# Reading the bias table back ahead of two weight preparations, and one weight remainder ahead of a residual update

## The reference

```python
h = h + 0.5 * swiglu(rms_norm(h, norm_ffn1), w_ffn1_in, w_ffn1_out)
u = rms_norm(h, norm_mix)
proj = u @ w_in
aq, ak, av, rq, rf, ri, rg, ga, gb = jnp.split(proj, splits, axis=-1)

# attention: 8 heads over a window of 128, with a bias by distance
bias = rel_table[bucket]                    # [128, 256, 8] from a [32, 8] table
s = jnp.where(valid, einsum(q, k) * 64 ** -0.5 + bias, -inf)
probs = exp(s - m) / (sum(exp(s - m)) + exp(sink - m));  att = probs @ v

# recurrence: f = lb + (1 - lb) * sigmoid(rf); S_t = diag(f_t) S_{t-1} + (1 - f_t) ri_t^T
rec = rms_norm(hgrn2(rq, rf, ri, lb), rec_norm) * sigmoid(rg)
merged = sigmoid(ga) * (att @ w_att_proj) + sigmoid(gb) * (rec @ w_rec_proj)
h = h + merged @ w_out
```

## Time and profile before

| | |
|---|---|
| median of three runs (lowest, highest) | 1578.72 us (1577.44, 1582.83) |
| the profiled execution's own time | 1577.44 us |
| its span in the trace | 1575.6 us |
| mean granted clock of TensorE | 0.962 of full speed |
| busy: TensorE, VectorE, ScalarE, GpSimd | 93%, 56%, 38%, 10% |

### The profile page before, as it was taken

How to read it: one execution, slowest core, us unless ns; L and a number is a source line. 1 busy time by engine, 2 the same in 40 slices (tenths; PEclk the granted TensorE clock), 3 DMA queues, 4 the chain that set the end, 5 groups by cost and what they waited for, 6 DMA issues and landing times.

```text
span 1575.6 us, 25429 instructions
## 1 busy us (share of the span) xinstructions
PE 1472.2 (93%) x10722; PEld 1385.5 (88%) x10722; DVE 879.6 (56%) x1154; ACT 595.4 (38%) x712; POOL 160.3 (10%) x149
## 2 busy tenths in 40 slices
PE   5999997899999999999989998999989889999997
PEld 5999997898899999988878878999988468999997
DVE  4656564674256565731564215866764263776765
ACT  3434343354034544421234112444442154444443
POOL 0000000132000000511011000000050042000014
PEclk9999998999999999999989769999999899999998
DMA  8555547632345555534300023555543412455540
GB/s 267 198 186 186 187 146 167 199 121 94 121 166 169 186 186 186 162 111 136 121 1 1 1 72 128 175 187 186 186 138 115 137 35 81 161 187 186 186 135 27
DMA packets 167216, 221.34 MB, mean 140 GB/s; under 512 B 5452, under 2 KB 148037, under 8 KB 167013
## 3 DMA queue, kind: packets, MB, share of 16 engines
q1 hardware_dynamic: 163564, 216.46, 41.8%
q10 hardware_dynamic: 3576, 3.81, 1.4%
HBM read 217.49 MB, written 2.62 MB: 140 GB/s over the span
## 4 chain that ended last, share of the span: by engine, by line
PE 80%; DVE 9%; ACT 4%; DMA 2%; issue 2%; POOL 1%; ACTq 0%; POOLq 0%; SPq 0%; DVEq 0%
PE ps L846 34%; PE ps L882 14%; PE ps L977 6%; PE ps L822 5%; DMA weight_bays<-in_w_in 2%; PE ps L959 2%; PE ps L1268 1%; PE ps L832 1%; DVE x_second_part L2038 1%; PE ps L1389 1%; PE ps L1405 1%; PE ps L806 1%; PE ps L1263 1%; PE ps L948 1%; PE ps L1417 1%
## 5 line engine op out<-in xcount | busy, mean ns | idle before, releaser
L2134 DVE TENSOR_TENSOR weights_second_parts<-weight_bays,weights_first_parts 128x2048 fp32r<-128x2048 f32 x132 | 301.0, 2289 | 172.4 <-ACT weights_first_parts L1526 172.0
L1526 ACT ACTIVATE weights_first_parts<-weight_bays 128x2048 fp32r<-128x2048 f32 x132 | 252.0, 1917 | 300.7 <-PE ps L846 190.1
L846 PE MATMUL ps<-x_first_part,weights_first_parts 128*128 128x256 f32 x1488 | 209.8, 284 | 1.7 <-DVE weights_second_parts L2134 1.7
L846 PE MATMUL ps<-x_second_part,weights_first_parts 128*128 128x256 f32 x1488 | 209.2, 284 | 0.0
L846 PE MATMUL ps<-x_first_part,weights_second_parts 128*128 128x256 f32 x1488 | 206.5, 282 | 0.0
L846 PEld LDWEIGHTS ps<-x_first_part,weights_first_parts 128*128 128x128 f32 x1488 | 191.3, 191 | 2.3 <-ACT weights_first_parts L1526 1.9
L846 PEld LDWEIGHTS ps<-x_second_part,weights_first_parts 128*128 128x128 f32 x1488 | 192.3, 191 | 0.0
L846 PEld LDWEIGHTS ps<-x_first_part,weights_second_parts 128*128 128x128 f32 x1488 | 189.6, 190 | 0.0
L882 PE MATMUL ps<-hidden_first_part,weights_first_parts 128*128 128x256 f32 x704 | 141.2, 282 | 5.4 <-ACT weights_first_parts L1526 3.7
L882 PE MATMUL ps<-hidden_second_part,weights_first_parts 128*128 128x256 f32 x704 | 141.2, 282 | 0.0
L882 PE MATMUL ps<-hidden_first_part,weights_second_parts 128*128 128x256 f32 x704 | 139.2, 278 | 0.0
(11 more groups left out here) (400 smaller groups left out, 2170.2 us busy)
## 6 DMA issues: line engine op xcount, KB each, us to landing
weight_bays<-in_w_ffn_in SPq DMA_DIRECT2D x44, 1024.0 KB, 5.1
weight_bays<-in_ffn_w_in SPq DMA_DIRECT2D x44, 1024.0 KB, 5.0
weight_bays<-in_w_ffn_out SPq DMA_DIRECT2D x22, 1024.0 KB, 5.0
weight_bays<-in_ffn_w_out SPq DMA_DIRECT2D x22, 1024.0 KB, 5.0
weight_bays<-in_w_in SPq DMA_DIRECT2D x19, 1024.0 KB, 5.7
weight_bays<-in_hyb_w_in SPq DMA_DIRECT2D x13, 1024.0 KB, 5.2
weight_bays<-in_ple_w_gate SPq DMA_DIRECT2D x8, 1024.0 KB, 5.2
weight_bays<-in_w_out SPq DMA_DIRECT2D x4, 1024.0 KB, 5.0
```

The costliest lines, as they stand in the source:

```text
L846: mm = nc.tensor.matmul(dst, w[:, k, j * P:(j + 1) * P], x[:, k], start=(n + k == 0), stop=(n == 2 and k == KD - 1))
L1526: nc.scalar.activation(hi, raw, ACT.Copy).then_inc(*w_hi_ready.inc(f, g, kind, of - g))
L2134: v.tensor_tensor(lo, raw, hi, ALU.subtract).then_inc(*w_lo_d.inc(f, g, kind, of - g))
```

## The change

Two sequences are written in another order; no instruction is added, removed or altered.

On ScalarE, in the body of `mix1`, the wait on `tab_out` and the two DMAs that read the bias back move from behind `prep(6)` and the keeping of ri's first half to ahead of `prep(4)`. On VectorE the remainder of chunk 1 moves from behind the mixer's factors to ahead of the update of h.

```diff
                     keep(fT[:, 2 * n:2 * n + 2], n, ("rf", n), "rf", n, func=ACT.Sigmoid)
-                prep(4)
-                prep(5)
-                prep(6)
-                keep(vR[:, :, 0:256], 0, ("ri", 0), "ri", 0)
                 act.wait_ge(tab_out.sem, 16)
                 shifted = [bass.AP(...) for o, n in ((0, 256), (P, P))]
                 act.dma_start(bias[:, :, 0:256], shifted[0]).then_inc(bias_in.sem, 16)
                 act.dma_start(bias[:, :, 256:384], shifted[1]).then_inc(bias_in.sem, 16)
-                prep(7)
-                keep(vR[:, :, 256:512], 1, ("ri", 1), "ri", 1)
+                prep(4)
+                prep(5)
+                for n in range(2):
+                    prep(6 + n)
+                    keep(vR[:, :, n * 256:(n + 1) * 256], n, ("ri", n), "ri", n)
                 act.wait_ge(*rec_d.at("f"))
...
             ffn("ffn1", False)
             rest_of_mix(0)
+            rest_of_mix(1)
             arrive("mix1", added("ffn1", 0.5, ("ffn1", 3 * GROUPS - 1)))
             factors("mix1", b=0)
-            rest_of_mix(1)
             split_x("mix1", lambda k: col("norm_mix", k), 1)
```

## The result

The changed kernel takes 1599.76 us, the median of four runs (1598.96 to 1600.10), against 1580.78 for the kernel before in the same comparison (1577.44 to 1585.67). The ratio is 1.0117, with a 95% interval of 1.0087 to 1.0147: slower by 19 us where 14.4 were forecast, and outside the range of 1587 to 1598. The profiled execution has 1596.38 us and a span of 1594.4, 18.8 more than the span of before, at a mean granted clock of 0.952 instead of 0.962.

The account below looks back on a forecast made before the run. TensorE's matmuls were taken to hold most of the chain, a weight chunk's landing 2%. ScalarE's 12.5 and VectorE's 1.9 us summed to +14.4, giving 1592.5 us from bases of 1577.44 and 1578.72; range 1587 to 1598.

Parts of the forecast that it names:

- The stop on ScalarE's wait: Ahead of `prep(4)`, ScalarE waits for the table's write until about 265.9 us; chunk 4 starts at 271.4; +12.5 us.
- The restart after a longer stop: Chunk 4, first after the stop, pays the low clock once as chunk 6 did: 7.67 us instead of 5.66.
- the third rival: At the restart in the mixer, the clock stays at 1.2 GHz for both ri chunks: 9.3 us more, 1601; 6%.
- Of this edit 1.85 us arrive at the end: VectorE's remainder of chunk 1 ahead of the update of h delays the table's write by 1.85 us.
- The base and the range: The +14.4 us was put on 1577.44 (profiled execution) and 1578.72 (median), giving 1592.5; range 1587 to 1598 us.
- +18: Upper end of the forecast's step once release, hand-overs, VectorE's term and restart vary; the lower end is +10.5.
- The first rival: The table's write ends sooner: break-even at 20 us; under about 10 us chunk 6's 8.7 us stop goes, 1571; 4%.
- No gain from reading early: Scores using the bias come after chunk 10 in both orders, so reading it back earlier serves nobody.
- +16.4: The sum if ScalarE's release came up to 2 us behind the write's last packet, by the skill's page; not adopted.

Follow-up runs that it names:

- e8_wait_only: The changed kernel with the two reads of the bias moved back behind ri's second half, the wait left ahead of `prep(4)`: 1597.79 us, ratio 1.0084.
- e7_wide_after: The changed kernel with the table's write made from 16 partitions in place of 8, the same bytes: 1579.87 us, ratio 0.9983 against the kernel before.
- e6_filled_less: The changed kernel with the embedding's second pair computed twice, filling TensorE's wait ahead of the sums: 1592.70 us, ratio 1.0065 against the kernel before.
- e4_wide_write: The kernel before with the table's write made from 16 partitions in place of 8, the same bytes: 1570.62 us, ratio 0.9923.

## Why the prediction was wrong in size and right in kind

- **The stop on ScalarE's wait: right.** Release, issues, preparation and restart came as written: 35.08 us from the write's issue to the read (34.99 in the row of before, and 34.87 to the release assumed), 1.15 for the issues and the hand-over (1.1), 4.38 to the first matmul (4.38), 7.52 for the first chunk (7.67). +12.54 for +12.5. `e8_wait_only` has the wait itself as the releaser, and in `e7_wide_after` the stop shrank by as much as the write.
- **The restart after a longer stop: right.** After 21 us of standing still the first chunk took 7.52 us, after 8.7 us 7.67, after 4.37 us (`e7_wide_after`) 7.26, where 5.66 is a chunk at full clock; the third rival falls. Its figure of 1601 is near the measured time by chance.
- **"Of this edit 1.85 us arrive at the end": the step that failed.** The term was mis-sized. The shift of the sums was there (TensorE waits 1.73 us for them), but the sum took the stretch behind it, of sums, bias product, embedding and spread, at the durations of one execution of before, in which the granted clock was 1.00 throughout. With the added wait it was 0.50, and the write went out 4.73 us late instead of 1.85. The filling that fitted (`e6_filled_less`) brought 2.87 of these back and put chunk 7 at +14.39, the sum as forecast. The same filling in VectorE's part alone took the start of chunk 6 from +4.53 to +1.81 us; its ratio went from 1.0031 to 1.0006, with intervals that overlap. The prediction named low clock as a cost of the big stop and never asked for it at the small one.
- **The base and the range: failed.** The forecast of +14.4 was put on 1577.44 and 1578.72. These are from the quicker group of executions of before; with 23 runs its median is 1585.31, and the change is worth 1.0096 (+15.3 us) against it. That this is close to the sum is luck: the sum lacks 2.9 us, and the median of before lies among its slower executions. By the lowest runs the change costs 18.5. The range allowed for runs between 1577.44 and 1582.83, the spread of three, not for a clock that takes 10 us from some executions and not from others. Its upper end is also below its own terms: +18 on 1582.83 is 1600.8, and the prediction gives no reason for stopping at 1598; the measured 1599.76 lies between. On that base, 1577.44 + 12.54 + 4.73 would have been 1594.7, and 5 us remain: 1.6 of low clock at 370 us, 0.6 in the rest of the first profile, and for what is left the second profile of the changed kernel shows low clock behind 800 us; it isn't accounted for piece by piece.
- **The first rival (a faster write): right in its price, wrong as an effect of the change.** The write didn't get quicker by itself. When it was made so (18.5 us, where the rival put the break-even at 20), a stop of 4.37 us remained and the time was 0.9983 of before, near the break-even. What it said of the old stop was too strict: the load of chunk 6 was to come free only with a write under about 10 us, and in `e4_wide_write` 18.5 were enough.
- **No gain from reading early: right.** Chunk 7 started without a gap, as in the earlier trace rows, and moving the reads back behind ri's second half (`e8_wait_only`) gave 1.0 us at chunk 4 and lost nothing that can be seen.

## What to carry to other kernels

A wait put earlier in an engine's order costs what is queued behind it, and its length must be read from the transfer it waits for, not from the waits that the profile shows: here a write of 35 us cost nothing before, because another wait covered it. A transfer's share of the engines tells whether it could be shorter: 41% of 16 engines for a queue with one transfer in it went with 8 engines, and a 16-row source was worth 8 to 12 us, where the new order of this change only cost. And a small added gap ahead of short products should be priced at both clock levels, with more than three runs of the base.

## What the runs showed of the hardware that wasn't expected

- A wait of 1.73 us ahead of the sums went with a granted clock of 0.50 (1.2 GHz) over 222 to 228 us; filling it with 1.7 us of repeated matmuls kept 1.00 in both profiles that had the filling fitted. The short products behind it were the same. Without wait and filling the clock held once and fell for a shorter time twice.
- Executions of one unchanged kernel on one core fall mostly into groups by mean clock, 1578 to 1579 us at 0.96 and 1585 to 1589 at 0.95, a spread of 0.7%; a few lie between.
- While the write held its 8 engines, a 1 MB load of SP's queue took 32.6 us to land; with the same bytes over 16 engines chunk 6's first part could start at 254.01 instead of 265.80.
- The Trainium skill's "DMA: Bandwidth & Descriptors" says, under Why a DMA increments its semaphore by 16 and not by 1, that the number of engines follows the slowest dimension of both access patterns, and, under Rules for kernel authors, that an outermost dimension under 16 confines a DMA. The traces agree: 8 closing packets and 41% with 8 rows, 16 and 79% with 16. The about 2 us that the same page, under Anatomy of one DMA, lays mostly to the receipt of the last byte isn't seen: about 0.5 us at most lay between the last packets and the read the earlier trace rows. The page gives that cost for DMAs issued from GpSimd, and this write was issued from ScalarE, which the prediction left out when it worked +16.4 out of it.
